# A two-layer encoder trunk on one core: another order for the opening, and a last product that ends tile by tile over five blocks

## The reference

```python
def swiglu(x, w1, w3, w2):
    return (jax.nn.silu(x @ w1) * (x @ w3)) @ w2

h = x
for layer in range(DEPTH):                 # DEPTH = 2
    if layer % 2 == 0:
        proj = h @ even_w_in[e]
        qa, ka, va, ub = jnp.split(proj, [MIX_A_WIDTH, 2 * MIX_A_WIDTH, 3 * MIX_A_WIDTH], axis=-1)
        oa = chunk_band_attention(qa, ka, va, even_rel_bias[e])
        ob = s5_mixer(ub, ssm_lambda_re[e], ssm_lambda_im[e], ...)
        mix = jnp.concatenate([oa, ob], axis=-1) @ even_w_out[e]
    else:
        qc, kc, vc = jnp.split(h @ odd_w_in[o], 3, axis=-1)
        mix = stick_breaking_attention(qc, kc, vc) @ odd_w_out[o]
    h = layer_norm(DEEPNORM_ALPHA * h + mix, ln_mix_g[layer], ln_mix_b[layer])
    ffn = swiglu(h, ffn_w1[layer], ffn_w3[layer], ffn_w2[layer])
    h = layer_norm(DEEPNORM_ALPHA * h + ffn, ln_ffn_g[layer], ln_ffn_b[layer])
```

## Time and profile before

| what | value |
|---|---|
| runs of the kernel | 1219.93, 1220.19, 1221.82 us; median 1220.19 us |
| the profiled execution | 1221.61 us, span in the trace 1219.8 us |
| mean granted TensorE clock | 0.995 |
| busy, share of the span | PE 98%, PEld 80%, POOL 43%, DVE 34%, ACT 34% |
| share of the chain that ended last | PE 90%, DVE 5%, ACT 2%, DMA 1%, issue 1% |

### The profile page before, as it was taken

The page is one execution under the profiler, slowest core; times in us unless marked ns, Lnnn a source line. Parts: engine busy times, 40 slices in busy tenths (PEclk is TensorE's granted clock), DMA queues, the critical chain, the costliest instruction groups (busy, mean ns, idle before and its releaser), DMA issues.

```text
span 1219.8 us, 14965 instructions
## 1 busy us (share of the span) xinstructions
PE 1190.9 (98%) x6221; PEld 970.4 (80%) x6221; DVE 410.4 (34%) x661; ACT 420.2 (34%) x577; POOL 522.1 (43%) x270
## 2 busy tenths in 40 slices
PE   7999999999999999999999999999999999999996
PEld 6887768988888888888887777667988888888885
DVE  8369452811111110000705877747211110110007
ACT  6344664332222322212235554523432232321220
POOL 6897514344444445443354223113544444444440
PEclk9999999999999999999999999899999999999999
DMA  8632315252333323323242211102533333323311
GB/s 211 180 88 72 103 43 198 69 145 87 104 101 89 104 87 103 104 88 103 94 120 84 65 53 55 50 8 79 158 102 90 100 104 88 102 91 102 102 52 69
DMA packets 152643, 117.30 MB, mean 96 GB/s; under 512 B 18689, under 2 KB 138537, under 8 KB 152577
## 3 DMA queue, kind: packets, MB, share of 16 engines
q1 hardware_dynamic: 152576, 116.36, 32.6%
HBM read 112.00 MB, written 3.17 MB: 94 GB/s over the span
## 4 chain that ended last, share of the span: by engine, by line
PE 90%; DVE 5%; ACT 2%; DMA 1%; issue 1%; POOL 0%; SPq 0%; DVEq 0%; ACTq 0%
PE ps L1473 17%; PE ps L1475 17%; PE ps L1474 17%; PE ps L1495 9%; PE ps L1496 9%; PE ps L1497 9%; PE ps L1918 2%; PE ps L1894 1%; PE ps L1905 1%; DMA raw<-in_even_w_in 1%; PE ps L1934 1%; PE ps L1503 1%; PE ps L1936 1%; PE ps L1935 1%; DVE stats L1347 1%
## 5 line engine op out<-in xcount | busy, mean ns | idle before, releaser
L567 POOL TENSOR_TENSOR wlo<-raw,whi 128x1024 fp32r<-128x1024 f32 x189 | 454.2, 2407 | 641.3 <-ACT whi L670 640.6
L1473 PE MATMUL ps<-xhi,whi 128*128 128x512 f32 (+1 forms) x1000 | 379.5, 379 | 0.9 <-ACT uP L714 0.9
L1475 PE MATMUL ps<-xhi,wlo 128*128 128x512 f32 (+1 forms) x1000 | 374.2, 374 | 0.0
L1474 PE MATMUL ps<-xlo,whi 128*128 128x512 f32 (+1 forms) x1000 | 374.2, 374 | 0.0
L670 ACT CAST whi<-raw 128x1024 fp32r<-128x1024 f32 x189 | 199.5, 1061 | 216.9 <-PE ps L1497 180.6
L1473 PEld LDWEIGHTS ps<-xhi,whi 128*128 128x128 f32 x1000 | 188.2, 188 | 42.2 <-issue 6.4
L1475 PEld LDWEIGHTS ps<-xhi,wlo 128*128 128x128 f32 x1000 | 188.3, 188 | 34.0
L1474 PEld LDWEIGHTS ps<-xlo,whi 128*128 128x128 f32 x1000 | 188.4, 188 | 32.2
L1016 DVE TENSOR_TENSOR gt<-ps,sg 128x512 f32<-128x512 f32 x44 | 30.4, 692 | 372.6 <-PE ps L1475 372.6
L1495 PE MATMUL ps<-whi,ghi 128*128 128x512 f32 x352 | 137.1, 390 | 0.0
L1497 PE MATMUL ps<-whi,glo 128*128 128x512 f32 x352 | 137.0, 389 | 0.0
(11 more groups left out here) (217 smaller groups left out, 1065.8 us busy)
## 6 DMA issues: line engine op xcount, KB each, us to landing
raw<-in_ffn_w SPq DMA_DIRECT2D x132, 512.0 KB, 3.7
raw<-in_odd_w_in SPq DMA_DIRECT2D x24, 512.0 KB, 3.9
raw<-in_even_w_in SPq DMA_DIRECT2D x16, 512.0 KB, 5.1
h<-in_x SPq DMA_DIRECT2D x8, 512.0 KB, 5.1
raw<-in_even_w_out SPq DMA_DIRECT2D x8, 512.0 KB, 3.7
raw<-in_odd_w_out SPq DMA_DIRECT2D x8, 512.0 KB, 3.6
bias<-rel_scratch SPq DMA_DIRECT2D x8, 256.0 KB, 4.2
out<-h SPq DMA_DIRECT2D x3, 512.0 KB, 2.6
```

What stands on the lines that cost most here:

```text
L567: eng.tensor_tensor(lo, raw_of(b), hi, ALU.subtract).then_inc(w_lo, 1)
L1473: eng.matmul(o_, w_hi_, x_hi_, start=start, stop=False)
L1474: eng.matmul(o_, w_hi_, x_lo_, start=False, stop=False)
L1475: return eng.matmul(o_, w_lo_, x_hi_, start=False, stop=stop)
```

## The change

It has two parts.

1. The opening. SP issues the first tile of x first and the eigenvalues behind it; of the small tables `b`, `rel` and `d` now come ahead of block 3, and `c` and `glu_b` between blocks 3 and 4. ACT rounds tile 0 of x ahead of the exponentials, tile 1, both halves of block 0 and tile 2 ahead of the sines, tile 3 behind them. DVE takes the four remainders of x spread through its argument chain, all of them ahead of the split of the angles. PE does `project_half(1)` before the angle products.
2. The last product. In the last call of `token_major` (norm_n 3) the tail that runs tile by tile has five blocks instead of four.

```diff
+LAST_TAIL = 5
...
             xt = x[0].rearrange("(t p) d -> t p d", p=P)
+            eng.dma_start(h[:, 0, :], xt[0]).then_inc(x_landed[0], 16)
+            eng.dma_start(dt2[:], log_dt[0].rearrange("(a b) -> a b", b=2)).then_inc(lam_landed, 16)
             eng.dma_start(pl[:, 7, :], lam_re[0].rearrange("(a b) p -> a (b p)", b=2)).then_inc(lam_landed, 16)
             eng.dma_start(pl[:, 8, :], lam_im[0].rearrange("(a b) p -> a (b p)", b=2)).then_inc(lam_landed, 16)
-            eng.dma_start(dt2[:], log_dt[0].rearrange("(a b) -> a b", b=2)).then_inc(lam_landed, 16)
-            eng.dma_start(h[:, 0, :], xt[0]).then_inc(x_landed[0], 16)
             eng.dma_start(h[:, 1, :], xt[1]).then_inc(x_landed[1], 16)
...
             weights_upto(3)
+            eng.dma_start(bnr[:], ...).then_inc(b_landed, 16)
+            eng.dma_start(bni[:], ...).then_inc(b_landed, 16)
+            eng.dma_start(reltab[:], rel[0]).then_inc(rel_landed, 16)
+            eng.dma_start(dd[:], ...).then_inc(d_landed, 16)
+            weights_upto(4)
             for dst, src in ((cdr, c_re), (cdi, c_im)):
...
-            eng.dma_start(reltab[:], rel[0]).then_inc(rel_landed, 16)
-            eng.dma_start(dd[:], ...).then_inc(d_landed, 16)
             eng.dma_start(glub[:], ...).then_inc(glub_landed, 16)
-            eng.dma_start(bnr[:], ...).then_inc(b_landed, 16)
-            weights_upto(4)
-            eng.dma_start(bni[:], ...).then_inc(b_landed, 16)
             weights_upto(6)
...
-                for k in range(k0, nk - TAIL):
+                tail = LAST_TAIL if norm_n == 3 else TAIL
+
+                for k in range(k0, nk - tail):
...
             project_half(0)
+            pe.wait_ge(x_ready, NT)
+            project_half(1)
             pe.wait_ge(ramp_ready, 2)
-            pe.wait_ge(x_ready, NT)
             for row, into in enumerate((angles, turns)):
...
             mm.then_inc(angle_done, 1)
-            project_half(1)
```

More of the change, by code:

```diff
@@ L423, in _ @@
             weights_upto(3)
+            eng.dma_start(bnr[:], b_re[0].rearrange("(a b) p i -> (b p) a i", b=2)).then_inc(b_landed, 16)
+            eng.dma_start(bni[:], b_im[0].rearrange("(a b) p i -> (b p) a i", b=2)).then_inc(b_landed, 16)
+            eng.dma_start(reltab[:], rel[0]).then_inc(rel_landed, 16)
+            eng.dma_start(dd[:], d_skip[0].partition_broadcast(GI)).then_inc(d_landed, 16)
+            weights_upto(4)
             for dst, src in ((cdr, c_re), (cdi, c_im)):
@@ L427, in _ @@
                         c_landed, 16)
-            eng.dma_start(reltab[:], rel[0]).then_inc(rel_landed, 16)
-            eng.dma_start(dd[:], d_skip[0].partition_broadcast(GI)).then_inc(d_landed, 16)
             eng.dma_start(glub[:], glu_b[0].rearrange("(t p) -> p t", p=P), allow_slow_non_contiguous=True).then_inc(glub_landed, 16)
-            eng.dma_start(bnr[:], b_re[0].rearrange("(a b) p i -> (b p) a i", b=2)).then_inc(b_landed, 16)
-            weights_upto(4)
-            eng.dma_start(bni[:], b_im[0].rearrange("(a b) p i -> (b p) a i", b=2)).then_inc(b_landed, 16)
             weights_upto(6)
@@ L691, in _ @@
             eng.activation(dt2[:], dt2[:], ACT.Exp).then_inc(dt_ready, 1)
+            upper_x(0, 0)
             act.wait_ge(m_ready, 1)
@@ L694, in _ @@
             eng.activation(scratch(MAG_), pl[:, 9, :], ACT.Exp).then_inc(mag_ready, 1)
+            upper_x(0, 1)
+            first_upper(0)
+            first_upper(1)
+            upper_x(0, 2)
             act.wait_ge(arg_ready, 1)
@@ L697, in _ @@
             eng.activation(pl[:, 17, :], pl[:, 13, :], ACT.Sin).then_inc(trig_ready, 1)
-            upper_x(0, 0)
-            first_upper(0)
-            upper_x(0, 1)
-            first_upper(1)
             rounded[0] = 1
-            upper_x(0, 2)
             upper_x(0, 3)
@@ L1067, in _ @@
             link(eng.tensor_scalar(q_(A), q_(A), ROUNDER, None, ALU.subtract))
+            lower_x(0, 0)
             for part in (TWO_PI_1, TWO_PI_2, TWO_PI_3):
@@ L1072, in _ @@
             eng.tensor_scalar(q_(RC), q_(RC), math.pi / 2, None, ALU.add).then_inc(arg_ready, 1)
+            lower_x(0, 1)
             count(tt(q_(A), q_(LR), q_(LR), ALU.mult))
@@ L1080, in _ @@
             count(eng.reciprocal(q_(A), q_(A)))
+            lower_x(0, 2)
             link(less(q_(TH8), q_(T), TWO_PI_1, q_(TH8)))
             link(less(scratch(TH8_), q_(T), TWO_PI_REST, q_(TH8)))
+            lower_x(0, 3)
             count(eng.tensor_scalar(scratch(TURN8_), scratch(TH8_), 1 / (2 * math.pi), None, ALU.mult))
-            lower_x(0, 0)
-            lower_x(0, 1)
             settle()
@@ L1089, in _ @@
             tt(turn_lo[:], both, turn_hi[:].bitcast(F32), ALU.subtract).then_inc(ramp_ready, 1)
-            lower_x(0, 2)
-            lower_x(0, 3)
             dve.wait_ge(mag_ready, 2)
@@ L1526, in token_major @@
                 for t in range(NT - 1):
-                    for k in range(nk - TAIL, nk):
+                    for k in range(nk - tail, nk):
                         if t == 0:
@@ L1532, in token_major @@
                         mm = token_rows(first + k, k, 0, D, hi, lo, t, 2 * t, 2, False, k == nk - 1)
-                        if t == 2 and k == nk - TAIL + 1 and norm_n < 3:
+                        if t == 2 and k == nk - tail + 1 and norm_n < 3:
                             turn_normed(norm_n + 1, 0)
                     mm.then_inc(acc_done, 1)
-                last_rows(first, range(nk - TAIL, nk), hi, lo, norm_n)
+                last_rows(first, range(nk - tail, nk), hi, lo, norm_n)
             def last_rows(first, ks, hi, lo, norm_n):
```

## The result

The changed kernel takes 1222.71 us (median of 15 runs, 1221.42 to 1225.91); measured beside it, the kernel before took 1220.70 (15 runs, 1219.11 to 1221.82). The ratio is 1.002, 95% interval 1.0012 to 1.0028: about 2 us slower, and outside the forecast range. The end gave what was forecast, about 1.7 us. So the opening, where a gain of 0.57 had been expected, must have lost some 3.7 us in the median; in the profiled execution it lost 2.3.

What follows compares the result with a forecast made beforehand. PE, busy 98% of the span, bounds the kernel, with DVE binding the end and transfers the first 12 us; 1.73 (end) plus 0.57 (opening) is 2.3 us, so 1220.19 - 2.3 = 1217.9 us, range 1216.8 to 1219.8.

Steps and rivals of the forecast that it cites:

- The opening: Stretch up to `project(2)`: reordered lists would start it at 27.35 instead of 27.92, a gain of 0.57 us.
- The end: Last product: with five tail blocks DVE waits for each tile instead of falling behind PE, a gain of 1.73 us.
- DVE's list: Opening: DVE's steps and four remainders of x, summed from the first cast, end at 16.3 and bind `project_half(1)`.
- ACT's list: Opening: tile 2 cast at 12.3, table load to 13.6, sines to 14.1, tile 3 cast at 15.1, just in time.
- The forecast's own condition for being wrong: Opening: the forecast is wrong if `project(2)` starts after 28; it was expected near 27.35.
- Tile 0 first: Opening transfers: tile 0 of x lands at 4.5 instead of 5.9, and what follows lands 0.5 us earlier.
- Rival 3: Opening: TensorE's clock still low in `project_half(0)`, which takes 5.8 instead of 2.9 us, to 18.0; 1219.5 us, chance 0.07.
- Rival 4: Opening: the table load on ACT costs twice its row, tile 3 cast at 16.4; 1219.1 us, chance 0.04.
- Rivals 1 and 2: Opening: weight block 4 lands at 25.3 to 27.6 (1219.0 us, chance 0.22) or after 27.6 (1223.0 us, chance 0.04).
- rival 1: Opening: block 4 lands at 25.3 to 27.6, `project(2)` starts 2.07 after it; middle 1219.0 us, chance 0.22.
- The angles: Opening: angles come 3.5 us later, DVE's work behind them 2.6 later, hidden in DVE's 2.90 us wait for `c`.

Runs made afterwards that it cites:

- e1: The kernel before with the five-block tail of the last product alone: 1219.28 us, ratio 0.9985.
- e16: The kernel before with the five-block tail alone, run again: 1219.04 us, ratio 0.9981.
- e18: The kernel before with the five-block tail alone, third time: 1219.14 us, ratio 0.9988.
- e5: The changed kernel with DVE's third remainder of x ahead of the two products and the fourth ahead of the reciprocal: 1228.77 us, ratio 1.0061.
- e9: The changed kernel with DVE's list alone put back in the order of before: 1221.48 us, ratio 0.9996.
- e12: The changed kernel with DVE's and PE's orders both put back: 1220.23 us, ratio interval 0.9987 to 1.0004.
- e13: e12 with ACT's table load and sines moved ahead of the cast of tile 1: 1220.01 us, ratio 0.9995.
- e11: The changed kernel with PE's order alone put back, angle products ahead of project_half(1): 1226.09 us, ratio interval 1.0025 to 1.0053.
- e6: The changed kernel with added unread transposes on PE ahead of tiles 0, 1 and 2 and between the projection halves: 1222.35 us, ratio interval 1.0002 to 1.0020.
- e15: e13 plus ACT's copy of the first projection ahead of block 4's rounding, plus added unread transposes ahead of tiles 0 to 2: 1219.69 us, ratio 0.9988.
- e7: The kernel before with the five-block tail and added unread transposes ahead of tiles 0 and 2: 1220.08 us, ratio interval 0.9984 to 1.0001.
- e10: The kernel before with PE's new order alone, project_half(1) ahead of the angle products: 1220.98 us, ratio interval 0.9992 to 1.0009.
- e3: The changed kernel with POOL waiting, ahead of block 0's low half, for DVE's steps of the argument chain: 1223.29 us, ratio 1.0022.

## Why the prediction was wrong

- **The end: right.** Forecast 1.73, measured 1.79 in the profile, and in the medians of the tail alone 1.67 (e1), 2.07 (e16) and 2.03 (e18). DVE idle ahead of tiles 1 and 2, and the second half 0.59 us behind PE (0.65 was in the sum).
- **DVE's list: the step that failed.** It was summed as "7.35 + 4.31 + 4 x 1.17 = 16.3", with 4.31 from rows of 5.73 to 10.04, where POOL stood idle (its memset ended at 5.61, its split began at 10.40). That DVE's steps would be spread over the time in which POOL splits block 0 was in the order; that they don't run there was not. Measured 19.38: of the 3.1 us too much, 2.63 are the stall (3.10 instead of 0.47), 0.3 a first cast that ended at 7.64, the rest small waits. The sign of it was in the trace of before, at 4.6 us, and was passed over: a step of DVE took 0.93 us where its like take 0.21, and ended with POOL's memset (timelines of POOL and DVE, kernel before). The step ahead of it took 0.60 beside the memset before that one.

```profile
4.60 1.01 POOL L547 MEMSET toep<- 128x1024 f32 x1
...
4.76 0.93 DVE L1067 TENSOR_SCALAR pl<-pl 16x128 f32<-16x128 f32 x1
```

- **ACT's list: a second term too small, hidden by the first.** Tile 3's cast was to be done at 15.1 and was at 16.29. ACT could take tile 1 only at 9.54, since it landed at 7.53 and was turned at half pace; from there ACT worked without a pause, so tile 2's cast ended at 13.58 instead of 12.3, and the load and the sines behind it took what was forecast. In this kernel it cost nothing, as DVE came later; without the stall (e5, e9) it alone puts the fourth remainder at 17.4 instead of 16.3. So the 0.57 wouldn't have come even with DVE at its usual pace.
- **`project_half(1)`** therefore began at 19.43 instead of 16.35, and `project(2)` at 30.42 instead of 27.35. The forecast's own condition for being wrong ("after 28") is met.
- **Tile 0 first.** It landed at 4.5 and was cast at 6.6, as forecast (6.3). But "what follows it lands earlier too", taken at 0.5 us, was wrong: tile 1 was there at 7.53 (issued at 2.63, 4.9 us to landing) and before at 7.45 (2.65 and 4.8), tile 2 at 10.5 in both, and the eigenvalues came at 5.2 instead of the 4.2 of the forecast. Moving one load ahead brought that load alone forward.
- **Rival 3 (the clock)** had 0.07 and 1219.5 us. Its mechanism came true: half pace until 16.6. That `project_half(0)` ended at 18.1, near its 18.0, is luck: it began at 13.9 and not at 12.2, and only half of it ran slowly. It was hidden behind DVE's lateness, so it cost nothing by itself in this kernel. Whether it is what keeps the opening at 51.1 to 51.8 with DVE undone (e9, e12, e13) isn't shown: the unchanged opening has 50.3 to 51.5 (e1, e16, e18). What had no place in the prediction is the half pace that can come back behind a pause, some 3 us lost in e5 and e11 and 1.7 in e6, none in e15. The rule of the Trainium skill cited there (TensorE: Matmul & The Clock Gate, Part 4: PE-mode transpose), that transposes don't raise the clock, fares no better with the runs: in e6 and e7 nothing but transposes had run when the pace doubled, between 6.9 and 8.0 and before 5.88.
- **Rival 4 (the table load)** is refuted again: it starts at 13.60 and the sine at 14.89, 1.29 us, against the page of the Trainium skill that it was drawn from (ScalarE: Activation LUTs, What ACT_TABLE_LOAD costs). **Rivals 1 and 2 (block 4)**: the condition of rival 1 came true. SP issued block 4 at 21.23 instead of 20.0, it landed near 26.4, later than the 25.3 that the forecast wanted, and the copy was done by 28.46. PE came later still. Block 4 alone would have given 28.5.
- **The angles.** 3.5 us later were to be hidden in DVE's wait of 2.90. They came 6.6 us later (24.45 against 17.8). That used up the wait, as DVE reached `c` at 37.59 without any, 0.7 us behind PE's transposes. It still cost nothing that PE shows: the transposes of `c` stand 5.5 us behind the start of `project(2)` in both kernels (27.92 to 33.54, 30.42 to 35.87), and `wnr` 17.2 behind those (50.78, 53.08). In e10, where the angles come 3 us later alone, nothing is lost either.

## What to carry to other kernels

A duration on DVE holds only for the neighbours it was measured with: before moving small SBUF steps to another time, lay POOL's timeline beside the new place. An idle gap of the engine that is the bound can cost more than its length, where its clock falls behind the gap (e5, e11; not in e15), so look at the granted clock behind every gap that a new order makes. And for a gain of 0.1%, compare stage by stage: here single executions of the same kernel jumped by 1.3 and 1.6 us in stages that no edit touched, and the granted clock of those stages told it each time.

## What the runs showed of the hardware

- Two operations of DVE on 16 x 128 values in SBUF took 3.10 us instead of 0.47 beside POOL's operation on 128 x 512 (1.5 us each); a single one of 0.29 took 2.89 beside POOL's 128 x 1024. Such a step ended 0.1 to 0.2 us behind POOL's instruction in the changed kernel, e3 and e5. The remainders of x (one operand from PSUM, result to SBUF, 128 x 1024) kept 1.2 us beside the same POOL operations.
- Not every such step is held: in the kernel before, two products at 3.61 kept 0.48 us beside POOL's memset (3.66 to 4.18), while steps with a single tensor as input took 0.60 and 0.93 instead of 0.21 beside the next two memsets; in e5 a step at 18.17, 0.10 us behind POOL's start, kept 0.22. All stalled steps beside POOL's splits read two tensors in SBUF.
- Before PE's pace has doubled for the first time, it can be half while the granted clock reads 1.00 (13.9 to 16.6 us in the changed kernel). Where it falls again afterwards, the record shows it: 0.73 in 10 to 15 us of e7, and 0.54 to 0.72 in 25 to 30 us of e3, e5, e6 and e11, with matmuls of 512 columns 0.43 us apart in e5.
- Half pace came back behind pauses of 1.15 us (e3), 1.59 (e7), 1.81 (e6), 1.90 (e5) and 3.69 (e11), and didn't behind 1.20 (changed kernel) nor behind 2.38 and 1.43 (e15): the length of the pause alone doesn't tell.
- With an unchanged opening the pace doubled at 10.57 in the kernel before, at 10.91 in e18 and only near 15.3 in e1: the moment isn't fixed by the program.
- Beside a 512 KB load issued ahead of them, the three small loads of the eigenvalues took 3.0 to 3.3 us to land, against 1.6 to 1.8 in the kernel before, where they came first.
